# Smaller pieces of the gated-linear-attention products, placed inside the projection's matmuls

## The reference, cut to what matters

```
def odd_mixer(h, w_in, w_gate_up, b_gate, norm_w, w_out):
    q, k, v, g, gk_low = _split(h @ w_in, ODD_IN_SIZES)
    glog = jax.nn.log_sigmoid((gk_low @ w_gate_up + b_gate).astype(f32)) / GLA_GATE_NORM
    ...
    o = chunk_gla(...)
    o = rms_norm(o, norm_w) * jax.nn.silu(g...)
    return o.reshape(b, l, GLA_VAL_DIM).astype(h.dtype) @ w_out

def chunk_gla(q, k, v, glog):
    bcum = jnp.cumsum(glog, axis=-2)
    q_dec = q * jnp.exp(bcum)
    attn = jnp.where(tri, jnp.einsum('bhnik,bhnjk->bhnij', q_dec, k * jnp.exp(-bcum)), 0.0)
    o_intra = jnp.einsum('bhnij,bhnjv->bhniv', attn, v)
    b_last = bcum[..., -1:, :]
    k_dec = k * jnp.exp(b_last - bcum)
    decay = jnp.exp(b_last[..., 0, :])
    def step(s, xs):
        qd, kd, vv, dl = xs
        o = jnp.einsum('bhik,bhkv->bhiv', qd, s)
        s = s * dl[..., :, None] + jnp.einsum('bhik,bhiv->bhkv', kd, vv)
        return s, o
```

## Time and profile before

| | us |
|---|---|
| median of three runs | 2170.39 |
| lowest and highest of them | 2167.16, 2171.52 |
| the profiled execution | 2170.83 |
| its span, first to last instruction | 2169.1 |
| TensorE busy in the span | 2137.7 (99%) |
| VectorE, ScalarE busy | 1009.3 (47%), 763.9 (35%) |
| granted TensorE clock, mean of the span | 0.996 |

### The profile page before, as it was taken

How to read it: one execution, slowest core, us unless ns; L and a number is a source line. 1 busy time by engine, 2 the same in 40 slices (tenths; PEclk the granted TensorE clock), 3 DMA queues, 4 the chain that set the end, 5 groups by cost and what they waited for, 6 DMA issues and landing times.

```text
span 2169.1 us, 38304 instructions
## 1 busy us (share of the span) xinstructions
PE 2137.7 (99%) x16006; PEld 2020.1 (93%) x16006; DVE 1009.3 (47%) x1390; ACT 763.9 (35%) x1259; POOL 100.1 (5%) x97
## 2 busy tenths in 40 slices
PE   8999999999999999999999999999999999999998
PEld 7999999998999999999999999999998788888887
DVE  6444422567585564443236444422663347444323
ACT  5322222436536442223234222322453454222222
POOL 0000000100060200000000000000000020000000
PEclk9999999999999999999999999999999999999999
DMA  4333342331110223234323233421331123333332
GB/s 127 94 96 87 96 119 77 83 79 50 50 31 2 86 80 96 87 88 124 90 58 88 87 95 89 119 84 52 94 83 55 42 72 92 97 90 94 97 107 78
DMA packets 328975, 179.69 MB, mean 83 GB/s; under 512 B 15850, under 2 KB 323345, under 8 KB 328879
## 3 DMA queue, kind: packets, MB, share of 16 engines
q1 hardware_dynamic: 327520, 175.30, 27.9%
q0 software_dynamic: 1024, 2.86, 0.6%
q10 hardware_dynamic: 334, 0.14, 0.0%
HBM read 176.16 MB, written 2.12 MB: 82 GB/s over the span
## 4 chain that ended last, share of the span: by engine, by line
PE 95%; DVE 3%; ACT 1%; DMA 0%; issue 0%; POOL 0%; SPq 0%; DVEq 0%; ACTq 0%
PE psum L608 70%; PE psum L620 10%; PE psum L834 6%; PE psum L2434 1%; DVE w_hl L523 1%; PE psum L2493 1%; PE psum L2978 1%; PE psum L1895 0%; DMA stage<-ffn_w_gate 0%; PE psum L2994 0%; PE psum L2989 0%; PE psum L1907 0%; DVE rinv L1411 0%; PE psum L711 0%; PE psum L687 0%
## 5 line engine op out<-in xcount | busy, mean ns | idle before, releaser
L608 PE MATMUL psum<-x_hl,w_hl 128*128 128x264 f32 (+1 forms) x9120 | 1242.0, 298 | 5.2 <-DVE w_hl L523 3.9
L608 PEld LDWEIGHTS psum<-x_hl,w_hl 128*128 128x128 f32 x9120 | 1182.5, 189 | 58.0 <-issue 6.7
L523 DVE TENSOR_TENSOR w_hl<-stage,w_hl 128x1024 fp32r<-128x1024 f32 (+1 forms) x310 | 396.5, 1279 | 348.7 <-ACT w_hl L516 348.7
L516 ACT ACTIVATE w_hl<-stage 128x1024 fp32r<-128x1024 f32 (+1 forms) x310 | 339.7, 1096 | 221.2 <-PE psum L608 92.0
L608 PE MATMUL psum<-acts,w_hl 128*128 128x264 f32 x2376 | 288.9, 284 | 0.0
L608 PEld LDWEIGHTS psum<-acts,w_hl 128*128 128x128 f32 x2376 | 288.6, 188 | 0.0
L1453 DVE TENSOR_TENSOR t_both<-psum,rinv 128x528 f32<-128x528 f32 (+1 forms) x88 | 61.9, 703 | 304.3 <-PE psum L608 304.3
L1254 ACT ACTIVATE acts<-t_both 128x528 f32 (+3 forms) x88 | 56.7, 644 | 400.3 <-DVE t_both L1456 400.3
L620 PE MATMUL psum<-x_hl,w_hl 128*128 128x264 f32 (+1 forms) x1344 | 172.2, 287 | 0.7 <-DVE w_hl L523 0.5
L620 PEld LDWEIGHTS psum<-x_hl,w_hl 128*128 128x128 f32 x1344 | 166.0, 188 | 2.7 <-DVE w_hl L523 0.9
L1447 DVE TENSOR_TENSOR t_both<-psum,rinv 128x528 f32<-128x528 f32 (+1 forms) x88 | 61.9, 703 | 181.7 <-PE psum L608 181.6
(11 more groups left out here) (350 smaller groups left out, 1290.7 us busy)
## 6 DMA issues: line engine op xcount, KB each, us to landing
stage<-ffn_w_gate SPq DMA_DIRECT2D x88, 512.0 KB, 3.8
stage<-ffn_w_up SPq DMA_DIRECT2D x88, 512.0 KB, 3.8
stage<-ffn_w_down SPq DMA_DIRECT2D x48, 704.0 KB, 4.7
stage<-odd_w_in SPq DMA_DIRECT2D x24, 512.0 KB, 3.8
stage<-ffn_w_down SPq DMA_DIRECT2D x22, 512.0 KB, 3.4
stage<-even_w_in SPq DMA_DIRECT2D x18, 512.0 KB, 4.0
stage<-even_w_out SPq DMA_DIRECT2D x8, 512.0 KB, 3.7
stage<-odd_w_out SPq DMA_DIRECT2D x8, 512.0 KB, 3.6
```

What stands on the lines that cost most here:

```text
L516: act.activation(weights(core.w_hl[:, slot.ring, 0, :], *kind), weights(core.stage[:, slot.stage, :], *kind), ACT.Copy).then_inc(core.w_hi, 1)
L523: dve.tensor_tensor(weights(core.w_hl[:, slot.ring, 1, :], *kind), weights(core.stage[:, slot.stage, :], *kind), weights(core.w_hl[:, slot ...
L608: op = pe.matmul(out, lhs, moving[:, moved, kt, t0:t0 + n], start=first and part + moved == 0, stop=last and part == 1)
```

## The change

Four things change. The gate products go into slot 6, one head behind each of the input tiles kt = 1, 3, 5 and 7, and use banks 2 to 5 alternately, so slot 8 no longer waits for them. The other pair goes to slots 5, 7, 9, 11 and 13. The state products now stand in three groups per head, (0, 1), (2, 3, 4, 5) and (6, 7); in the second the row halves alternate (64 to 127, 0 to 63, and again), and `KV_PLACES` puts neighbours into different banks. The groups are no longer back to back: some stand between slots (`KV_BETWEEN`), some inside a slot behind its third input tile (`KV_INSIDE`, `KV_INSIDE_KT = 2`), that is, behind 18 of its 48 matmuls. VectorE's steps follow in `STATES_AT` and `STATES_LATE_AT`.

```diff
-    other = s == RING + 1 or (phase.layer == 1 and GATES_OUT < s < KEYS_FROM and s % 2 == 0)
+    other = s == RING + 1 or (phase.layer == 1 and GATES_OUT < s < KEYS_FROM and s % 2 == 1)
...
-                if phase.layer == 1 and slot.local == GATES_OUT + 2:
-                    pe.wait_ge(k.odd.s_gate_x, GH)
...
+            elif phase.mix is not None:
+                odd_tensor_inside(k, pe, phase.mix, slot.local, kt)
...
-GATE_AT = {GATES_OUT - 1: [0, 1, 2], GATES_OUT: [3]}
+GATE_AT = {GATES_OUT: range(GH)}
...
-KV_FIRST_AT = {18: 0, 19: 1, 21: 2, 23: 3}
+KV_BETWEEN = {18: [(0, 1)], 19: [(1, 0)], 20: [(1, 2)], 21: [(2, 0)], 22: [(2, 2)], 23: [(3, 0)], 24: [(3, 2)]}
+KV_INSIDE = {18: [(0, 0)], 19: [(0, 2)], 20: [(1, 1)], 22: [(2, 1)], 24: [(3, 1)]}
+KV_INSIDE_KT = 2
+STATES_AT = {17: [(0, 0)], 18: [(0, 1), (0, 2)], 19: [(1, 0)], 21: [(2, 0)], 23: [(3, 0)]}
+STATES_LATE_AT = {19: [(1, 1)], 20: [(1, 2)], 21: [(2, 1)], 22: [(2, 2)], 23: [(3, 1)], 24: [(3, 2)]}
 VALUES_AT = {17: 0, 18: 1, 20: 2, 22: 3}
-KV_REST_AT = {18: 0, 20: 1, 22: 2, 24: 3}
...
-KV_GROUPS = ((0, 1), (2, 4), (3, 5), (6,), (7,))
-KV_FIRST, KV_REST = range(0, 3), range(3, 5)
-KV_BEFORE = (0, 0, 2, 5, 6)
+KV_GROUPS = ((0, 1), (2, 3, 4, 5), (6, 7))
+KV_BEFORE = (0, 2, 6)
+KV_PLACES = ((0, 0), (0, 1), (1, 0), (0, 0), (1, 1), (0, 1), (1, 0), (0, 0))
...
+def gate_products(k, o, pe, mix, h):
+    if h == 0:
+        pe.wait_ge(k.scaled, mix.evac0 - ODD_TILES - 1 + RING)
+        pe.wait_ge(o.s_in, 48)
+    if h >= 2:
+        pe.wait_ge(o.s_gate_x, h - 1)
+    for b, (t0, n) in enumerate(halves(FULL)):
+        op = pe.matmul(k.psum[:, 2 + 2 * (h % 2) + b, 0:n], o.gate_up[:, h * P:(h + 1) * P],
+                       o.proj[0:RANK, GATE_LOW, t0:t0 + n], start=True, stop=True)
+    op.then_inc(o.s_gate_lin, 1)
...
+def odd_tensor_inside(core, pe, mix, s, kt):
+    k, o = core, core.odd
+    if s == GATES_OUT and kt % 2:
+        gate_products(k, o, pe, mix, kt // 2)
+    for h, g in KV_INSIDE.get(s, []):
+        if kt == KV_INSIDE_KT:
+            head_products(k, o, pe, h, g)
...
 def kv_bank(k, n_chunk):
-    g = kv_group(n_chunk)
-    at = KV_GROUPS[g].index(n_chunk) * VD
-    return k.psum[:, g % 2, at:at + VD]
+    bank, side = KV_PLACES[n_chunk]
+    return k.psum[:, bank, side * VD:(side + 1) * VD]
```

More of the change, by code:

```diff
@@ L2888, in odd_tensor_between @@
     ps, proj = k.psum, o.proj
[L2889 to L2898, removed]
     for c in KEYS_AT.get(s, []):
@@ L2918, in odd_tensor_between @@
         head_outputs(k, o, pe, OUT_AT[s])
-    if s in KV_FIRST_AT:
-        head_products(k, o, pe, KV_FIRST_AT[s], KV_FIRST)
     if s in VALUES_AT:
         head_values(k, o, pe, VALUES_AT[s])
-    if s in KV_REST_AT:
-        head_products(k, o, pe, KV_REST_AT[s], KV_REST)
+    for h, g in KV_BETWEEN.get(s, []):
+        head_products(k, o, pe, h, g)
     if s in TURN_AT:
@@ L2964, in head_values, with head_products @@
     op.then_inc(o.s_v_flip, 1)
-def head_products(k, o, pe, h, groups):
+def head_products(k, o, pe, h, g):
     pe.wait_ge(o.s_v_set, h + 2)
     pe.wait_ge(o.s_k_set, NBLK + 1)
[L2972 to L2980, removed]
+    if STATES * h + KV_BEFORE[g]:
+        pe.wait_ge(o.s_state, STATES * h + KV_BEFORE[g])
+    for n_chunk in KV_GROUPS[g]:
+        c, r0, t0, n = CHUNKS[n_chunk]
+        rows = slice(r0, r0 + n)
+        op = pe.matmul(kv_bank(k, n_chunk), o.k_rows(c)[rows, h, :], o.v_rows[rows, c, h * VD:(h + 1) * VD],
+                       start=True, stop=True)
+    op.then_inc(o.s_kv_made, 1)
 def head_outputs(k, o, pe, h):
@@ L3027, in odd_scalar_between @@
         act.wait_ge(o.s_gate_lin, h + 1)
-        act.activation(token_cols(o.ex[:, h, :], FULL), bank_cols(k, h % 3, FULL), ACT.Identity,
+        act.activation(token_cols(o.ex[:, h, :], FULL), bank_cols(k, 1 + h % 2, FULL), ACT.Identity,
                        bias=k.vec_cols[:, 48 + h:49 + h]).then_inc(o.s_gate_x, 1)
@@ L3144, in odd_vector_between @@
                               ALU.mult).then_inc(o.s_attn_set, 1)
-    if s in KV_FIRST_AT:
-        head_states(k, o, dve, KV_FIRST_AT[s], range(0, 6))
+    for h, g in STATES_AT.get(s, []):
+        head_states(k, o, dve, h, KV_GROUPS[g])
     if s in OUT_AT and s <= ODD_LAST:
         head_inverse(o, dve, OUT_AT[s])
-    if s in KV_REST_AT:
-        head_states(k, o, dve, KV_REST_AT[s], range(6, STATES))
+    for h, g in STATES_LATE_AT.get(s, []):
+        head_states(k, o, dve, h, KV_GROUPS[g])
     if s in TURN_AT:
```

## The result

The changed kernel takes 2159.76 us (median of five runs, 2157.41 to 2162.08) against 2170.39 us before (median of five). The ratio is 0.995, with a 95% interval of 0.9939 to 0.9962: 8 to 13 us less. The profiled execution took 2158.23 us, with a span of 2156.5 us against 2169.1.

The account below looks back on a forecast made before the run. TensorE, holding 95% of the chain that ended last, was taken to bound the kernel. State products 4.5, gate products 0.3, pairs 1.05 and clock 6.4 sum to 12.3 us; from 2170.83 this gives 2158.5 us, range 2155.5 to 2165.

Parts of the forecast that it names:

- The waits: TensorE's waits in layer 1's mixer: 3.2 us for VectorE's state chain, 0.9 and 0.8 for evacuations, expected to go.
- The charge of 0.2 to 0.3 us in slot 19: Remaining wait of TensorE for VectorE's states ahead of head 0's group (6, 7), charged at 0.2 to 0.3 us.
- State products: Slots 18 onward, regrouped: 1.06 us saved in each of three heads, 1.57 in head 0; net 4.5 us.
- the entry into a narrow block: Going from a slot to narrow products was priced at 0.09 us each.
- my price list: Distances between starts at full clock, such as 5.91 us for a slot behind products.
- Why the pairs run together: Middle group's two pairs take 1.06 us because every neighbour is in the other half and the other bank.
- Gate products and pairs: Gate products in slot 6 save 0.3 us; the other pair at odd slots removes slot 14's wait, 1.05 us.
- The clock: Two low-clock stretches behind narrow blocks with a wait in the middle, 3.3 and 3.1 us, both go: 6.4 us.
- the spread of the runs: Executions before, 2167.16 to 2171.52 us, were said to differ by about one low-clock stretch.
- Rival 1: One low-clock stretch stays or appears, most likely in slot 6 or at slot 20: 2161.7 us, chance 0.18.
- rival 2: Pairs in the group of four do not run together, or breaking up blocks costs more: 2161.9 us, chance 0.08.
- Rivals 3 and 4: 3: clock ignores waits, two low stretches stay, 2164.9 us, chance 0.07; 4: six low stretches, 2177.7 us, chance 0.03.

Follow-up runs that it names:

- kv_back: The changed kernel with the state products as before: five groups, the first three back to back; median 2167.54 us, ratio 0.9987 to the kernel before.
- experiment 7: The changed kernel with the middle state group in the order 2, 4, 3, 5; median 2162.4 us, ratio 0.9953 to the kernel before.
- experiment 3: The changed kernel with the other pair of PSUM banks at even slots 8, 10 and 12 as before; median 2161.43 us, ratio 0.9956.
- narrow_long: The changed kernel with chunk 0's 16-row product made nine times instead of once for every head; median 2187.72 us, ratio 1.0067.
- experiments 1, 5: 1: kv_back. 5: waits for the state chain filled with unused full-width products, in the kernel before (2171.99 us) and in kv_back (2166.06 us).
- experiment 6: The run narrow_long: 16-row product of chunk 0 made nine times per head in the changed kernel; 2187.72 us.
- experiments 4, 8: 4: front_back. 8: the changed kernel again, 2161.24 us, then with outputs grouped, 2158.48, and value transposes moved inside three slots, 2157.29, or two, 2153.74.
- front_back: The changed kernel with everything ahead of slot 15 (gate products, pairs, slot 8's wait) as before; median 2159.92 us, ratio 0.996.

## Why the prediction was right, and where it was off

The forecast was 2158.5 us and 12.3 us of gain. The profiled execution took 2158.23, and the median is 2159.76, 1.3 above the forecast; it moved by 10.6.

- **The waits** went as said: 3.2, 0.9 and 0.8 us left the list. The charge of 0.2 to 0.3 us in slot 19 was right in kind: from 1654.43 to 1656.94 us are 2.51, where the same 18 matmuls of slot 20 take 2.36.
- **State products**, 4.5 us forecast: the stretch lost 10.5 us, less the forecast's own 6.4 for the clock 4.1, and kv_back gave 4.2. The term that was mis-sized is the entry into a narrow block. I charged 0.09 us per block inside a slot. Slot 20's own matmuls take 2.36 + 3.73 = 6.09 us, against 5.91 undivided, so each costs 0.18: the way back into the slot costs as much as the way out. I had missed it because the 5.91 us of my price list is a slot behind products and holds one way back already: eight slots without a break take 46.50 us, 5.81 each. Five such blocks make the 0.4 us.
- **Why the pairs run together** I had wrong, with no harm to the number: alternation is not needed, only that both halves stand in one group with no wait between (experiment 7).
- **Gate products and pairs**, 1.35 us forecast, 1.24 measured. The pairs alone are 1.13 (experiment 3), so the gates' new order is worth 0.1 at full clock rather than 0.3. Four ways back into a slot where there were two, 0.18 us that I had not charged, explain that.
- **The clock**, 6.4 us forecast. Both low stretches went, and the mixer's clock was full in both profiles of the changed kernel. It was full around the state products in all eight traces with the new order, narrow_long aside, and fell in all three that kept open waits. That the block with a wait in its middle was the place is shown: filling the wait removed the falls, and rebuilding the block brought one back (experiments 1, 5). That the wait was needed is refuted (experiment 6). I also read the spread of the runs as one stretch in this mixer, more or less. Falls in layer 0, which no edit touches, and behind the gate products (experiments 4, 8) spread them too.
- **The median** moved 1.7 us less than forecast and 2.0 less than the profiled pair of executions. 0.9 us of that pair's 12.6 were outside the mixer. The rest depends on how often each kernel's clock falls, which one trace of a kernel does not say. By the medians the clock gave 10.6 - 4.1 - 1.24 = 5.3 us (an estimate), not 6.4. And here luck helped the forecast: nine of the fourteen traces have one to three falls of 3.4 us in layer 0, but neither the one from which I started nor the one that it is held against has any.
- Rival 1, a fall in slot 6 or at slot 20, was not seen in any trace with the new order and the products as they are; rival 2 fell with the 1.13 us rows, though its second half, that blocks cost more than I charged, holds for the 0.4 us above. Rivals 3 and 4 fell with the clock.

## What to carry to other kernels

Read the granted clock by stretch as well as the waits: a wait at or inside a block of narrow products (few rows) costs its own length and, in some executions, 1.5 to 3.3 us more for the clock. Put narrow products into the middle of a dense slot, far enough ahead of whoever must answer them; one such place costs 0.18 us, and moving transposes away can open a wait elsewhere, so look at who stood behind them. Group products of one shape: that was worth 2.9 us here for a reordered loop.

## What the hardware showed that I had not expected

- A fully busy TensorE can lose its clock: four falls inside or at the end of blocks of 3.4 us more of 16-row products in narrow_long, with no wait in any block. In front_back it was busy for 3.50 of 3.50 us ahead of the fall, but a wait of 0.80 us had ended just before them. The low stretches were 3.4, 6.8 or 10.2 us long; one of 3.4 cost 1.5 to 1.6 us and one of 6.8 about 3.2.
- Products in rows 0 to 63 and in rows 64 to 127 behave as two streams: in the order 2, 4, 3, 5 all four take 1.14 us, as in the alternating order, and two of one half alone take 1.13.
- Each change between the `128*128` and the `128*64` products of a head's output costs more than I had read off the starts: four changes fewer per head saved 0.72 us, 0.18 each, the same as a narrow block in a slot.
